# A one-core transformer kernel: opening, loads, seams, query rotation, and mask and scores ahead of the turning

## The chip, the cores and the metric

The kernel runs on one core of one Trainium2 chip. The metric is the device time of one execution in microseconds; lower is better. Engines are TensorE (PE; its weight loads are shown as PEld), VectorE (DVE), ScalarE (ACT), GpSimd (POOL) and SyncE (SP). They run at once, each in the order of its own program, and wait for one another by semaphores.

## The reference

The input is one sequence of 512 tokens with 1024 features. The reference computes a chain of blocks, each with a residual: an HGRN mixer, a SwiGLU feed-forward, sparse attention (NSA) on shared keys and values, a second SwiGLU, and then a second stage with differential attention, a squared-ReLU feed-forward, a state-space layer (S5) and another feed-forward. The first layers are modulated: the condition c goes through silu and a matrix into gains and shifts.

```python
def modulate(x, gain, shift, scale):
    return rms_norm(x, gain) * (1 + scale[:, None, :]) + shift[:, None, :]
# NSA: q, keys and values by head; rope on q and on two of three key sets
s_c = einsum('bqhgd,bchd->bhgqc', qp, kc) * scale      # against compressed blocks
s_s = einsum('bqhgd,bqhkd->bhgqk', qr, ks_g) * scale   # against selected blocks
s_w = einsum('bqhgd,bkhd->bhgqk', qr, kw) * scale      # against a window
o = g[:, :, 0] * o_c + g[:, :, 1] * o_s + g[:, :, 2] * o_w
```

Compressed keys and values come from a two-layer MLP over blocks of 32 tokens (cmp_w1, cmp_w2). With 512 tokens all eight selectable blocks are selected and the window covers the sequence, so both are causal attentions.

## The kernel before

Activations lie transposed: 8 tiles of 128 features by 512 tokens. Every large product is computed as three products of rounded parts: weights are split into whi (ScalarE, a rounding copy, L388) and wlo (VectorE, the rest, L392), activations into hh and hl. Weights come in blocks of 1 MB on SP's queue, two buffers deep. A *segment* is one matrix (h_q, h_f, h_v, h_g, h_out, ffn0_in0, ...); its blocks are processed in turn, and each engine has a body per block. PSUM banks 0 to 3 serve two blocks alternately. Between two segments whose results are taken by different engines, `boundary` on TensorE waits until every result of the segment before has been taken: ahead of the first block (L2665) where the new segment reads the same activations, behind it (L2677) where it waits for new ones.

The modulation columns of later layers are computed alongside: for each block ScalarE issues a load into `ada_ring` (L489), VectorE adds eight slices weighted by silu(c) (`ada_sums`, L509 and L513), and TensorE sums over partitions (`ada_products`, L473). In a segment's last block `ada_sums` goes before the eviction, and `ada_products` before the sums of squares.

*Opening.* Modulation columns of the first norm: 8 slices of ada_w (SP's queue). VectorE accumulates 12 of 16 columns (L527, L530), TensorE computes 4 by 128x1 products (L547) and closes the 12 by 12 products with ones (L559). x comes last on ScalarE's queue (2 MB). TensorE turns it (L2632); ScalarE squares (L2185) and copies (L2186) each turned tile; TensorE sums squares with a matrix of ones (L538). The gain, the norm's factor and the shift give hh and hl.

*NSA projections.* Segments n_kvc (2 blocks), n_ks, n_vs, n_kw, n_vw (1 each), n_q (4). Before n_kvc ScalarE issues `nsa_loads` (L655 to L667): rope tables, masks, gate weights, both cmp_w1 (2 MB each) and cmp_w2. Hooks `n_hook_pe`, `n_hook_act`, `n_hook_dve` run after block nb (n_kvc 0 and 1, n_ks 2, n_vs 3, n_kw 4, n_vw 5, n_q 6 to 9). POOL swaps half heads by small DMAs for the rotation.

*Query rotation.* Queries are eight tiles, in four pairs. `query_pieces(b)` are five VectorE steps on 1024 columns (L754, L757, L761, L766, L769): times sine, times cosine, add, times the norm's factor, and the same factor on the unrotated query. Pairs 0, 1, 2 run in the hooks 7, 8, 9, and the five pieces of pair 3 in attention steps 4 to 8. The factor of all lies in `xn`.

*Attention.* 68 steps: per key head one compressed step and two query pairs x four token tiles (t = 3 to 0) x two branches, with (t+1) x 128 keys. Step w consists of mask (L869) and scores (L887; L881 for compressed) on TensorE, a maximum on VectorE (L1113), exp on ScalarE (L1007), weighting on VectorE (L1100), turning on TensorE (L899), a copy on ScalarE (L995, L991), and products with values on TensorE (L919). They are pipelined: in iteration w TensorE does turn(w-3), mask(w), scores(w), values(w-4). Scores alternate between two bank pairs, so mask(w) waits for exp(w-2); the turned tiles have one bank pair, so turn(w) waits for copy(w-1). ScalarE does copy(w-3), then exp(w); VectorE maximum(w), then weighting(w-1).

## Time and profile before

| | |
|---|---|
| median of 3 runs | 2970.71 us (2970.0 to 2975.85) |
| the profiled execution's own time | 2976.58 us |
| its span, first to last instruction | 2974.8 us |
| PE busy (share of the span) | 2788.4 us (94%) |
| DVE busy | 1643.8 us (55%) |
| ACT busy | 1059.9 us (36%) |
| POOL busy | 100.4 us (3%) |
| chain that ended last | PE 62%, issue 23%, DVE 9%, DMA 3%, ACT 2% |
| mean granted TensorE clock | 0.971 |

All views are of the one profiled execution, and times inside are counted from its first instruction. Matmul busy times overlap a little, since they are pipelined: "busy" for TensorE is an upper figure. A row of the timeline ends, where the engine stood idle before it, with the idle time and what ended it. "L899" is line 899 of the kernel; tiles that were carved out of one tensor have its name (nsa_area, s_area, h_area).

### The profile page before, as it was taken

How to read it: one execution, taken by the hardware profiler on the slowest of the kernel's cores; microseconds unless marked ns; L12 is line 12 of the kernel's file. 1: busy time of each engine (PE TensorE's matmuls, PEld its weight loads, DVE VectorE, ACT ScalarE, POOL GpSimd, SP SyncE). 2: the span in 40 equal slices, each digit the busy share in tenths (PEclk: the TensorE clock that was granted, in tenths of full speed). 3: DMA queues.
4: the chain of work that ended last, by engine and by line, in shares of the span. 5: the costliest groups of instructions: out<-in, count | busy, mean ns of one | idle time of the engine just before them, and what ended most of it. 6: DMA issues, size and time to landing. Idle time of an engine off the chain costs nothing.

```text
span 2974.8 us, 38309 instructions
## 1 busy us (share of the span) xinstructions
PE 2788.4 (94%) x14746; PEld 2238.9 (75%) x14746; DVE 1643.8 (55%) x2350; ACT 1059.9 (36%) x1559; POOL 100.4 (3%) x135
## 2 busy tenths in 40 slices
PE   5999999999979899999999998899999968999999
PEld 4898778888668556788887775788887757778787
DVE  4566566766436776533334557477777394353342
ACT  3312233222323565332233448332341524342231
POOL 2004000000011000000000100000000000000000
PEclk9999999999989999999999999999999988999999
DMA  5640346565363100333333420144444661323232
GB/s 209 199 148 1 105 136 198 149 197 157 105 182 107 43 1 15 97 88 96 94 87 110 126 79 1 57 101 134 141 143 150 231 108 64 92 85 99 85 99 71
DMA packets 402088, 326.36 MB, mean 110 GB/s; under 512 B 14920, under 2 KB 387360, under 8 KB 400928
## 3 DMA queue, kind: packets, MB, share of 16 engines
q1 hardware_dynamic: 319936, 232.80, 26.7%
q10 hardware_dynamic: 77376, 80.07, 8.4%
q0 software_dynamic: 4640, 11.60, 1.5%
q8 instruction: 95, 1.56, 0.2%
q14 instruction: 41, 0.34, 0.0%
HBM read 293.05 MB, written 19.86 MB: 105 GB/s over the span
## 4 chain that ended last, share of the span: by engine, by line
PE 62%; issue 23%; DVE 9%; DMA 3%; ACT 2%; POOL 1%; ACTq 1%; DVEq 0%; POOLq 0%
PE ps L451 44%; PE ps L429 3%; PE ps L445 2%; PE ps L433 1%; DVE ada_acc L1781 1%; DMA ada_ring<-in_ada_w 1%; PE ps L899 1%; DVE ada_ring L513 1%; PE ps L919 1%; PE ps L1649 1%; PE ps L2648 1%; PE ps L887 1%; DVE h_area L1783 1%; DVE h_area L1785 1%; DMA xin<-in_x 1%
## 5 line engine op out<-in xcount | busy, mean ns | idle before, releaser
L451 PE MATMUL ps<-hh,whi 128*128 128x512 f32 x1744 | 693.5, 398 | 5.0 <-DVE xT L2484 1.6
L451 PE MATMUL ps<-hh,wlo 128*128 128x512 f32 x1744 | 681.7, 391 | 0.0
L451 PE MATMUL ps<-hl,whi 128*128 128x512 f32 x1744 | 681.1, 391 | 0.0
L392 DVE TENSOR_TENSOR wlo<-raw,whi 128x2048 fp32r<-128x2048 f32 x198 | 453.9, 2292 | 364.7 <-ACT whi L388 364.7
L388 ACT ACTIVATE whi<-raw 128x2048 fp32r<-128x2048 f32 x198 | 377.6, 1907 | 381.5 <-PE ps L451 250.9
L451 PEld LDWEIGHTS ps<-hh,whi 128*128 128x128 f32 x1744 | 329.1, 189 | 80.0 <-issue 11.9
L451 PEld LDWEIGHTS ps<-hl,whi 128*128 128x128 f32 x1744 | 329.2, 189 | 71.6 <-issue 4.5
L451 PEld LDWEIGHTS ps<-hh,wlo 128*128 128x128 f32 x1744 | 328.8, 189 | 69.7
L451 PE MATMUL ps<-hid_h,whi 128*128 128x512 f32 x756 | 306.7, 406 | 0.0
L451 PE MATMUL ps<-hid_l,whi 128*128 128x512 f32 x756 | 298.4, 395 | 0.0
L451 PE MATMUL ps<-hid_h,wlo 128*128 128x512 f32 x756 | 298.4, 395 | 0.0
L451 PEld LDWEIGHTS ps<-hid_h,whi 128*128 128x128 f32 x756 | 141.8, 188 | 37.8 <-issue 4.3
L451 PEld LDWEIGHTS ps<-hid_l,whi 128*128 128x128 f32 x756 | 141.8, 188 | 37.4 <-issue 4.3
L451 PEld LDWEIGHTS ps<-hid_h,wlo 128*128 128x128 f32 x756 | 141.7, 187 | 34.6
L513 DVE SCALAR_TENSOR_TENSOR ada_ring<-ada_ring,cact 128x256 f32<-128x256 f32 (+1 forms) x336 | 151.8, 452 | 12.1
L2227 ACT ACTIVATE sq<-xT 128x512 f32 (+1 forms) x56 | 35.4, 632 | 292.8 <-DVE xT L2484 139.4
L2482 DVE TENSOR_TENSOR xT<-xT,ps 128x512 f32 (+1 forms) x40 | 27.4, 687 | 163.1 <-PE ps L451 142.6
L2290 ACT ACTIVATE hid_h<-hid_f 128x512 f32 (+1 forms) x44 | 27.8, 633 | 246.9 <-DVE hid_f L2530 246.9
L2368 ACT ACTIVATE act_t<-ps 128x512 f32<-128x512 f32 x64 | 38.0, 598 | 198.4 <-PE ps L451 189.5
L429 PE MATMUL ps<-hh,whi 128*128 128x512 f32 x176 | 77.1, 438 | 32.6 <-ACT hh L2210 32.6
L2582 DVE TENSOR_TENSOR hid_f<-act_t 128x512 f32<-128x512 f32 x64 | 43.5, 688 | 102.8 <-ACT act_t L2368 102.4
L2530 DVE TENSOR_TENSOR hid_f<-act_t,ps 128x512 f32<-128x512 f32 x44 | 30.2, 686 | 126.6 <-PE ps L451 121.7
(413 smaller groups left out, 4076.0 us busy)
## 6 DMA issues: line engine op xcount, KB each, us to landing
raw<-in_ffn_w_in SPq DMA_DIRECT2D x44, 1024.0 KB, 6.0
ada_ring<-in_ada_w ACTq DMA_DIRECT2D x82, 512.0 KB, 4.4
raw<-in_ffn_w_up SPq DMA_DIRECT2D x32, 1024.0 KB, 5.3
raw<-in_ffn_w_down SPq DMA_DIRECT2D x32, 1024.0 KB, 5.6
raw<-in_ffn_w_out SPq DMA_DIRECT2D x32, 704.0 KB, 4.5
raw<-in_hgrn_w_in SPq DMA_DIRECT2D x16, 1024.0 KB, 5.6
raw<-in_attn_w_qkv SPq DMA_DIRECT2D x12, 1024.0 KB, 5.1
s_area<-cp_dram SPq DMA_DIRECT2D x6, 2048.0 KB, 9.0
```

The lines of the kernel that those rows point to most:

```text
L388: nc.scalar.activation(whi[:, par, :], raw[:, par, :], ACT.Copy).then_inc(w_hi, 1)
L392: nc.vector.tensor_tensor(wlo[:, par, :], raw[:, par, :], whi[:, par, :].bitcast(F32), ALU.subtract).then_inc(w_lo, 1)
L429: nc.tensor.matmul(ps[:, 2 * par + j, :], tile(w, kt, j), hi[:, kt, :], start=(kt == 0 and n == 0), stop=False)
L433: m = nc.tensor.matmul(ps[:, 2 * par + j, :], tile(wh, kt, j), lo[:, kt, :], start=False, stop=(kt == k - 1))
L445: m = nc.tensor.matmul(ps[:, bank, half * 256:half * 256 + 256], x[:, kt, t0:t0 + P], w[:, kt, :], start=(kt == 0 and n == 0), stop=(kt == ...
L451: m = nc.tensor.matmul(ps[:, bank, :], tile(w, kt, j), x[:, kt, :], start=(kt == 0 and n == 0), stop=(kt == k - 1 and n == 2))
L513: nc.vector.scalar_tensor_tensor(out=acc if last else w[:, 0, :], in0=w[:, kt, :], scalar=cact[:, kt:kt + 1], in1=w[:, 0, :], op0=ALU.mult ...
L887: m = nc.tensor.matmul(ps[:, S_BANK[w % 2] + i, 0:n], nqr[rows, p, t * P:(t + 1) * P], (k_sel, k_win)[br][rows, p // 2, 0:n], start=False, ...
L2227: nc.scalar.activation(sq[:, q:q + 1, :], xT[:, bass.ds(b * s.dve + j, 1), :], ACT.Square).then_inc(sq_rdy, 1)
L2368: nc.scalar.activation(act_t[:, j, :], ps[:, 2 * par + j, :], ACT.Relu).then_inc(ev_a, 1)
L2530: nc.vector.tensor_tensor(hid_f[:, par, :], act_t[:, par, :], ps[:, 2 * par + 1, :], ALU.mult).then_inc(ev_v, 1)
L2582: nc.vector.tensor_tensor(hid_f[:, j, :], act_t[:, j, :], act_t[:, j, :], ALU.mult).then_inc(hidf_rdy, 1)
```

## The change

1. *Opening.* x is loaded first, on SP's queue. TensorE turns x first, with the narrow products of slices 0 and 1 between. Squares are taken from the untransposed x by ScalarE, one row per token with a running sum (`accum_out`); VectorE spreads the four columns over a diagonal after its fourth slice, and TensorE sums with four 128x128 products. The closing products are split: 4 columns for the gain first, then 8 for the shift in another bank. VectorE computes the gain, two normalised tiles, then shift and the first wlo.
2. *Loads.* Both cmp_w1 and cmp_w2 leave `nsa_loads` and are issued after block 1 of n_kvc.
3. *Seams.* `boundary` is always put behind the first block of a segment; before it, only evictions up to the last block are awaited. In the last block of a segment with a norm behind it `ada_sums` goes behind the eviction, and `ada_products` behind the sums of squares.
4. *Query rotation.* Pair 1 runs in hook 9, pairs 2 and 3 in attention steps 1 to 10, and the factors lie in separate places.
5. *Attention.* In iteration w mask and scores go ahead of the turning.

```diff
@@ ada_first_dve, behind the slice kt
+                if kt == 3:
+                    first_square_spread(dve)
...
+        def first_square_spread(dve):
+            for t in range(TT):
+                dve.wait_ge(x_sq, t + 1)
+                nc.vector.tensor_scalar(rstd[:, t * P:(t + 1) * P], ident[:, :], x_ssq[:, t:t + 1], None, ALU.mult
+                                        ).then_inc(sq_rdy, 2)
+        def first_square_sums(pe):
+            for t in range(TT):
+                pe.wait_ge(sq_rdy, 2 * t + 2)
+                nc.tensor.matmul(ps[:, 7, t * P:(t + 1) * P], ones[:, :], rstd[:, t * P:(t + 1) * P], start=True, stop=True,
+                                 skip_group_check=True).then_inc(ssq_rdy, 2)
...
-            for j in range(NV):
-                m = nc.tensor.matmul(ps[:, 4, j:j + 1], ada_sum[:, j * P:j * P + P], ones[:, 0:1],
-                                     start=False, stop=True, skip_group_check=True)
-            m.then_inc(ada0_used, 1)
+            for bank, part in ((4, range(KT, NV)), (6, range(KT))):
+                for j in part:
+                    m = nc.tensor.matmul(ps[:, bank, j:j + 1], ada_sum[:, j * P:j * P + P], ones[:, 0:1],
+                                         start=(j == 0), stop=True, skip_group_check=True)
+                m.then_inc(ada0_used, 1)
@@ head_rstd
-            if n >= 6:
-                act.wait_ge(hn_rdy, n)
+            if n == 8:
+                act.wait_ge(hn_rdy, 6)
...
+        Q_RS = [xn[:, :, :], nqr[:, 4:6, :], xn[:, :, :], sq[:, :, :]]
@@ attention_pe
-                if w == 3:
-                    pe.wait_ge(ev_a, after(seg["n_q"])[1])
-                if 0 <= w - 3 < NS:
-                    turn(w - 3)
                 if w < NS:
...
                     scores(w)
                 if w == 1:
                     last_query_sums()
+                if w == 3:
+                    pe.wait_ge(ev_a, after(seg["n_q"])[1])
+                if 0 <= w - 3 < NS:
+                    turn(w - 3)
@@ n_hook_act
+            if nb == 1:
+                cmp_loads(act)
@@ nsa_act, before the copy of step 2
+                    if w == 5:
+                        act.wait_ge(hn_rot, 10)
@@ n_hook_dve
-            if nb >= 7:
-                for piece in query_pieces(dve, nb - 7):
+            if nb in (7, 9):
+                for piece in query_pieces(dve, (nb - 7) // 2):
                     piece()
@@ nsa_dve
-                if 4 <= w < 9:
-                    last_query[w - 4]()
+                if 1 <= w < 11:
+                    last_queries[w - 1]()
@@ ScalarE, opening
-                if kt >= 2:
-                    act.wait_ge(ssq_rdy, kt - 1)
-                nc.scalar.activation(sq[:, kt % 2, :], ps[:, kt % 4, :], ACT.Square).then_inc(sq_rdy, 1)
                 nc.scalar.activation(xT[:, kt, :], ps[:, kt % 4, :], ACT.Copy).then_inc(ev_v, 1)
+                if kt % 2:
+                    t = kt // 2
+                    if t >= 2:
+                        act.wait_ge(x_sq, t - 1)
+                    nc.scalar.activation((sq, xn)[t % 2][:, :, :].rearrange("p s n -> p (s n)"), xin[:, t, :], ACT.Square,
+                                         accum_out=x_ssq[:, t:t + 1]).then_inc(x_sq, 1)
@@ VectorE, linear
-                    ada_sums(dve, s, b, par)
+                    late = s.name in norm_after and isinstance(b, int) and b == s.n - 1
+                    if not late:
+                        ada_sums(dve, s, b, par)
                     evac(b, par)
+                    if late:
+                        ada_sums(dve, s, b, par)
@@ TensorE, linear
-                if change and need is None:
-                    boundary(pe, s)
-                elif change:
+                if change:
...
-                    if change and need is not None and isinstance(b, int) and b == 1:
+                    if change and isinstance(b, int) and b == 1:
                         boundary(pe, s)
```

On ScalarE, in the order of its program, this stands before n_kvc and in it before the change (L489 is the modulation load, L2249 the eviction, L388 the rounding of a weight block):

```order
L657 DMA nsa_area<-in_k_rope 128x1280
L658 DMA nsa_area<-in_k_nsa 128x772
L659 DMA nsa_area<-in_nsa_w_q 128x8x48
L661 DMA nsa_area<-in_cmp_w 128x16x256
L662 DMA nsa_area<-in_cmp_w 128x16x256
L664 DMA nsa_area<-in_cmp_w 128x2x64 x2
L666 DMA nsa_area<-in_cmp_w 128x2x64
L489 DMA ada_ring<-in_ada_w 128x8x128
L2249 ACTIVATE nsa_area<-ps 128x512 x2
L388 ACTIVATE whi<-raw 128x2048
```

And this after the change, down to the eviction of n_ks (L2344, L2345):

```order
L672 DMA nsa_area<-in_nsa_w_q 128x8x48
L489 DMA ada_ring<-in_ada_w 128x8x128
L2275 ACTIVATE nsa_area<-ps 128x512 x2
L388 ACTIVATE whi<-raw 128x2048
L489 DMA ada_ring<-in_ada_w 128x8x128
L2275 ACTIVATE nsa_area<-ps 128x512 x2
L388 ACTIVATE whi<-raw 128x2048
L677 DMA nsa_area<-in_cmp_w 128x16x256
L678 DMA nsa_area<-in_cmp_w 128x16x256
L680 DMA nsa_area<-in_cmp_w 128x2x64 x2
L682 DMA nsa_area<-in_cmp_w 128x2x64
L2344 ACTIVATE sq<-ps 128x512
```

Five issues have moved from ahead of the first modulation load to behind n_kvc's second conversion and ahead of n_ks's eviction.

On TensorE two iterations of the attention (t falls from 3 to 0; L899 turns, L869 is the mask, L887 scores, L919 values) read before:

```order
L899 MATMUL ps<-ident,nsa_area 128x128 x6
L869 MATMUL ps<-mask_r 128x128 x2
L887 MATMUL ps<-nsa_area 128x256 x2
L919 MATMUL ps<-nsa_area 64x128 x8
L899 MATMUL ps<-ident,nsa_area 128x128 x6
L869 MATMUL ps<-mask_r 128x128 x2
L887 MATMUL ps<-nsa_area 128x128 x2
L919 MATMUL ps<-nsa_area 64x128 x6
```

And after, with L887 the mask, L905 scores, L917 the turning and L937 values:

```order
L887 MATMUL ps<-mask_r 128x128 x2
L905 MATMUL ps<-nsa_area 128x128 x2
L917 MATMUL ps<-ident,nsa_area 128x128 x6
L937 MATMUL ps<-nsa_area 64x128 x6
L887 MATMUL ps<-mask_r 128x128 x2
L905 MATMUL ps<-nsa_area 128x128 x2
L917 MATMUL ps<-ident,nsa_area 128x128 x4
L937 MATMUL ps<-nsa_area 64x128 x6
```

The turning now stands between the scores of a younger step and the values of an older one.

On VectorE, from the attention's first maximum on (L1113; L1100 weights, L754 is a step of pair 3), before:

```order
L1113 TENSOR_REDUCE nsa_area<-ps 128x2
L1096 RECIPROCAL nsa_area<-nsa_area 128x2
L1097 TENSOR_TENSOR nsa_area<-nsa_area 128x2
L1100 TENSOR_SCALAR nsa_area<-nsa_area 128x384 x2
L754 TENSOR_TENSOR h_area<-h_area,nsa_area 128x1024
```

And after, one iteration of the second step of the attention (L1135 is the maximum, L1122 weights, L775 is a step of pair 2):

```order
L1135 TENSOR_REDUCE nsa_area<-ps 128x2
L1118 RECIPROCAL nsa_area<-nsa_area 128x2
L1119 TENSOR_TENSOR nsa_area<-nsa_area 128x2
L1122 TENSOR_SCALAR nsa_area<-nsa_area 128x512 x2
L775 TENSOR_TENSOR nsa_area<-nsa_area 128x1024
```

The rotation steps begin in iteration 1 instead of 4 and there are ten of them instead of five.

## Rows read from the trace of the kernel before

**Rows 1.** Timeline, opening: start, duration, engine, line, operation, operands, count, idle before, releaser

```profile
15.01 0.46 PE L2625 MATMUL ps<-ident,vec_a 120*128 120x120 f32 x1 [15.01 <-DMA ones<-in_k_ones]
...
29.99 1.82 DVE L530 SCALAR_TENSOR_TENSOR ada_sum<-ada_first,cact,ada_sum 128x1536 f32<-128x1536 f32 x1 [1.34 <-DMA ada_first<-in_ada_w]
...
31.00 0.59 ACT L2186 ACTIVATE xT<-ps 128x512 f32<-128x512 f32 x1
...
47.49 5.26 PE L559 MATMUL ps<-ones,ada_sum 128*128 128x1 f32 x24
...
53.13 2.28 DVE L392 TENSOR_TENSOR wlo<-raw,whi 128x2048 fp32r<-128x2048 f32 x1
...
57.04 0.77 PE L429 MATMUL ps<-hh,whi 128*128 128x512 f32 x1 [4.30 <-ACT hh L2210]
```

**Rows 2.** Stretches: length, busy PE PEld DVE ACT POOL, clock, DMA share, GB/s

```profile
16.00:29.00 13.00, 3.58 (x16) 3.49 (x16) 11.93 (x7) 1.31 (x2) 0.00 (x0) 1.00 1.01 414
```

**Rows 3.** Timeline of the key/value projections: DMA issues and waits behind them

```profile
828.27 7.89 ACTq L664 DMA_DIRECT2D nsa_area<-in_cmp_w  x2
...
836.87 1.17 ACTq L489 DMA_DIRECT2D ada_ring<-in_ada_w  x1
...
844.24 0.28 DVE L509 TENSOR_SCALAR ada_ring<-ada_ring,cact 128x128 f32<-128x128 f32 x1 [20.52 <-DMA ada_ring<-in_ada_w]
...
852.41 0.58 PE L473 MATMUL ps<-ones,ada_acc 128*128 128x1 f32 x2 [4.53 <-DVE ada_acc L513]
```

**Rows 4.** Stretch in TensorE's pause, columns as in rows 2

```profile
842.00:844.00 2.00, 0.00 (x0) 0.00 (x0) 0.00 (x0) 1.98 (x2) 0.00 (x0) 0.50 1.04 272
```

**Rows 5.** Stretches: first and second group of the sparse attention

```profile
992.00:1036.60 44.60, 39.28 (x314) 25.21 (x314) 34.93 (x87) 30.84 (x83) 0.00 (x0) 0.89 0.01 1
1036.60:1081.20 44.60, 40.95 (x380) 27.32 (x380) 31.79 (x88) 30.41 (x85) 0.00 (x0) 1.00 0.01 1
```

**Rows 6.** TensorE's waits in the second group: sum us, times, longest us

```profile
PE ps L899 <- ACT nsa_area L995: 1.8, 4, 0.7
PE ps L899 <- ACT nsa_area L991: 1.2, 1, 1.2
PE ps L899 <- DVE nsa_area L1087: 0.7, 1, 0.7
```

**Rows 7.** Timeline of ScalarE, a 1024-wide activation of the query norm

```profile
957.82 1.06 ACT L726 ACTIVATE xn<-xn 128x1024 f32<-128x1024 f32 x1
```

**Rows 8.** Chain of waits, n_ks and n_kw on TensorE: start, us, what

```profile
852.99 13.76 PE ps L451 x48
...
881.50 10.91 PE ps L451 x48
```

**Rows 9.** Chain of waits at a seam, from mlp0_out0 to mlp0_in1

```profile
2783.81 3.05 PE ps L451 x13
...
2788.13 1.90 PE ps L451 x7
```

**Rows 10.** Timeline of VectorE at the end of h_out

```profile
419.99 1.41 DVE L2445 SCALAR_TENSOR_TENSOR xn<-xT,gains_a,rstd 128x512 f32<-128x512 f32 x2
```

**Rows 11.** Timeline at the attention's start and in its first steps

```profile
990.96 0.68 DVE L1074 TENSOR_REDUCE nsa_area<-ps 128x16 f32<-128x512 f32 x1
...
1001.09 1.09 PE L899 MATMUL ps<-ident,nsa_area 128*128 128x128 f32 x8 [2.70 <-ACT nsa_area L991]
...
1004.02 0.96 DVE L1113 TENSOR_REDUCE nsa_area<-ps 128x2 f32<-128x768 f32 x1 [3.44 <-PE ps L887]
...
1005.95 1.22 DVE L754 TENSOR_TENSOR h_area<-h_area,nsa_area 128x1024 f32<-128x1024 f32 x1
```

**Rows 12.** Chain of waits: widest values, turn and scores at full clock

```profile
1094.33 1.07 PE ps L899 x8
...
1097.19 1.02 PE ps L919 x16
...
1105.56 1.06 PE ps L887 x4
```

More of the change, by code:

```diff
@@ L531, in ada_first_dve @@
                                                    op0=ALU.mult, op1=ALU.add).then_inc(ada0_sum_v, 1)
+                if kt == 3:
+                    first_square_spread(dve)
             dve.wait_ge(cols_ps, 2)
             link(nc.vector.tensor_copy(cols_b[:, 0:NROW_B], ps[:, 5, 0:NROW_B]))
-        def first_square_sum(pe, kt):
-            pe.wait_ge(sq_rdy, kt + 1)
-            nc.tensor.matmul(ps[:, 7, :], ones[:, :], sq[:, kt % 2, :], start=(kt == 0),
-                             stop=(kt == KT - 1)).then_inc(ssq_rdy, 1)
+        x_ssq = gains_a[:, 4, 0:TT]
+        def first_square_spread(dve):
[8 more added lines that the diff above has]
+                                 skip_group_check=True).then_inc(ssq_rdy, 2)
         def ada_first_pe(pe, k0, k1):
@@ L787, in n_hook_pe @@
                 pe.wait_ge(ada_rdy, seg["n_kvc"].ada_seg + 1)
-                pe.wait_ge(nsa_in, 64)
+                pe.wait_ge(nsa_in, 48)
                 head_square_sums(pe, 0, after(seg["n_ks"])[1])
@@ L966, in n_hook_act @@
                 nc.scalar.activation(gates.rearrange("p t n -> p (t n)"), ps[:, 7, 0:192], ACT.Copy).then_inc(gate_rdy, 1)
-                head_rstd(act, 6, xn[:, :, :])
+                head_rstd(act, 6, Q_RS[1])
             if nb == 9:
-                head_rstd(act, 8, xn[:, :, :])
+                head_rstd(act, 8, Q_RS[2])
         def nsa_act_seam(act, link):
@@ L1010, in nsa_act @@
                 if w == 2:
-                    head_rstd(act, 10, xn[:, :, :])
+                    head_rstd(act, 10, Q_RS[3])
         def nsa_dve_round(dve):
@@ L1032, in n_hook_dve @@
             if nb == 2:
-                dve.wait_ge(nsa_in, 64)
+                dve.wait_ge(nsa_in, 48)
                 link(nc.vector.tensor_reduce(small[:, 1:2], rotm, AX.X, ALU.add))
@@ L1101, in weighted @@
                 ins.then_inc(at_p, 1)
-            last_query = query_pieces(dve, 3)
+            last_queries = query_pieces(dve, 2) + query_pieces(dve, 3)
             for w in range(NS + 5):
@@ L1153, in d_hook_pe @@
             if db == 1:
-                pe.wait_ge(nsa_in, 96)
+                pe.wait_ge(nsa_in, 80)
             if 1 <= db <= 8:
@@ L1291, in diff_dve_start @@
             s = ROWS["attn_subln_2"]
-            dve.wait_ge(nsa_in, 96)
+            dve.wait_ge(nsa_in, 80)
             lv = lam_vec.rearrange("p (a b n) -> p a b n", a=2, b=2)
@@ L2086, in _ @@
         def _(sp):
+            sp.dma_start(xin[:, :, :], a["x"][0].rearrange("(t p) d -> p t d", p=P)).then_inc(x_in, 16)
             for kt in range(FIRST):
@@ L2423, in _, with first_shift @@
             dve.wait_ge(cols_rdy, 1)
-            link(nc.vector.tensor_tensor(mods[:, 0:16], ps[:, 4, 0:16], cols_a[:, 0:16], ALU.add))
-            modulated_gain(0, ROWS["norm_mix"], 8).then_inc(mods_rdy, 1)
-            if upto >= 2:
+            link(nc.vector.tensor_tensor(mods[:, 8:16], ps[:, 4, 8:16], cols_a[:, 8:16], ALU.add))
+            link(modulated_gain(0, ROWS["norm_mix"], 8))
+            def first_shift():
+                dve.wait_ge(ada0_used, FIRST + 2)
+                nc.vector.tensor_tensor(mods[:, 0:8], ps[:, 6, 0:8], cols_a[:, 0:8], ALU.add).then_inc(mods_rdy, 1)
                 convert_lo(dve, segs[0], 0, 0, 0)
@@ L2447, in apply @@
                                                    op0=ALU.mult, op1=ALU.mult).then_inc(xn_rdy, 1)
+                    if j == 0 and kt == 1:
+                        first_shift()
                     if kt:
@@ L2498, in _ @@
             if upto >= 2:
-                dve.wait_ge(mods_rdy, 1)
                 apply(0, 0, *mod_cols(0), FIRST_UNITS)
@@ L2631, in _ @@
                 for t in range(TT):
-                    m = nc.tensor.transpose(ps[:, kt % 4, t * P:(t + 1) * P], xin[:, t, kt * P:(kt + 1) * P],
-                                            ident[:, :])
+                    m = nc.tensor.transpose(ps[:, kt % 4, t * P:(t + 1) * P],
+                                            xin[:, t, kt * P:(kt + 1) * P], ident[:, :])
                 m.then_inc(mm, 1)
-                if kt:
-                    first_square_sum(pe, kt - 1)
-            first_square_sum(pe, KT - 1)
+                if kt % 4 == 3:
+                    ada_first_pe(pe, kt // 4, kt // 4 + 1)
+            ada_first_pe(pe, 2, 4)
+            first_square_sums(pe)
             def square_sums(s, m, b, par):
```

24 lines of the change are left out of this document (12 added, 12 removed).

## The prediction, made before the changed kernel was run

> **What bounds the kernel now.** I read the page's engine shares, then the chain of waits, then the stretches where TensorE stands still, and in those the timeline of all engines. TensorE is busy for nearly the whole span, so only time in which it waits, or runs at the lower clock, can be won. The change touches four such places.
>
> In the opening TensorE does not start the first weight block until 57.04 [rows 1]. Between 16 and 29 us the DMA engines move 414 GB/s [rows 2], so the stretch ends with a transfer: VectorE adds the last of eight slices of the first modulation weights at 29.99. All else follows serially: x is turned, squared and summed on TensorE, and only then come the 24 narrow products from 47.49 to 52.75, a full VectorE conversion (53.13 to 55.41), and the first products.
>
> In the key/value projections ScalarE stands at its own DMA issues, 7.89 us for one line. The modulation load behind them is issued at 836.87, VectorE waits 20.52 us for it, and TensorE resumes at 852.41 [rows 3], having fallen to half the clock while it stood (0.50, that is 1.2 GHz [rows 4]).
>
> Between segments with different evacuators TensorE waits for the last eviction. In the sparse attention it is busy 40.95 of 44.60 us in a steady group [rows 5], and its waits there stand before the turning [rows 6].
>
> **The opening.** x moves to the head of SP's queue, its turning goes before the weight products, squares are taken row by row on ScalarE, and only 4 of 12 late columns are wanted before the gain. The first 30 us still carry the same bytes: x (2.1 MB) and eight slices (8.4 MB), 10.5 MB, which at 414 GB/s is 25.4 us; with about 2 us until the first data and as much for landing the last slice is there at about 29.4. It was used at 29.99. So the last VectorE addition ends at about 31.4, or later if something else stops VectorE: the new spread of squares stands after its fourth slice. ScalarE needs for it eight copies at about 0.5 apart and four squares of 1024 columns with their sums, about 1.25 each by the 1.06 of a 1024-wide activation [rows 7], 9.0 us together, starting some 2.4 us after the constants land. If they land at 12 instead of 15, squares end at 23.4, the spread at 24.3, four additions of 1.82 later it is 31.7. If at 15, 34.7. I take 31.7, since x's small rows now precede the large ones. Then 8 of the 24 narrow products (5.26/24 = 0.22 each) make 1.8, the two VectorE steps 0.5: gain at 34.0. Two normalisations run while the other 16 products end at 37.0. The shift and the conversion (2.28) end at about 39.8, where 55.41 stood. The move of the conversion behind two normalisations costs nothing, since it waits for the shift anyway. The products, whose high parts are then there, and VectorE's first low part start at about 39.9, where TensorE started at 57.04 and the low part at 56.9: 17.0, of which I take **16.5 us**, as the constants may be a little later than 12. Bounds: 13 (constants at 15) and 19 (nothing but the last slice binds).
>
> **The loads.** The two large compression weights and three small ones leave ScalarE's queue ahead of n_kvc and are issued after its second block. Left ahead are three loads; the first modulation load is issued at 824 instead of 836.87 and lands behind 1.25 MB at about 831. Then 2.9 us of VectorE sums, 2.3 of conversion for n_ks, 2.9 of the second sums: 839.2, and the product. n_ks starts at 839.7 instead of 852.99: 13.3. It needs 11.0, about what n_kw takes at full clock (10.91), instead of 13.76 [rows 8], if TensorE stands only 2 us: 2.8. Two waits for ScalarE's evictions (n_vs, n_vw) go, 2.5 as two seams of 1.27 [rows 9]. Together **18.6 us**. The moved issues hold ScalarE for about 10 to 12 us from 843 on. Behind them stand n_ks's evictions and the conversion for n_kw. TensorE meanwhile runs n_ks to 850.7 and, as it no longer waits for those evictions, n_vs to 862.5 and its sums to 864.2. By my bookkeeping ScalarE is free at about 856, n_kw's low weights are there at 862.8: 1.4 us spare. If that cover is gone, each us late is a us lost; bounds 11 and 20. Compression's own weights are wanted by VectorE only at about 872.
>
> What speaks against it is contention: the rows show ScalarE held until 836.87 while 4.2 MB move [rows 3], and now POOL's 2 MB of copies and n_kw's 1 MB of weights start inside the same stretch.
> The Trainium skill (DMA: Bandwidth & Descriptors, "Issuing engines are not separate DMA queues") says that transfers of all issuing engines run on the same 16 DMA engines and interleave. By that rule the moved bytes delay n_kw's weights, and the term would be some 4 us smaller; without it 18.6 stands. The same rule leaves the last opening slice where it is. By that rule 414 GB/s is what all queues share; the trace agrees, with a DMA share of 1.01 in that stretch [rows 2].
>
> **Segment seams.** Outside the NSA part the wait for all evictions moves behind the first block for h_v, ffn0_in1, ffn1_in1, d_v and both second mlp inputs. A seam of this kind is 2786.86 to 2788.13, 1.27 us [rows 9]; I count 1.3, 0.7, 1.5, 1.0, 1.3, 1.3: **7.1 us**, bounds 4 and 8. In h_out the last eviction goes ahead of 4.1 us of modulation sums that now run beside the squares; but VectorE still has sums, conversion (2.29) and then the gain in a row from about 411.4: normalising at 418.2 instead of 419.99 [rows 10]: **1.8 us** (0 to 4). In n_out TensorE's last block binds: nothing.
>
> **Query rotation.** Of twenty full-width VectorE steps of 1.22, before the attention now stand those of query pair 1 where those of pair 2 stood, so it still starts at the same point relative to the projection (990.96 before [rows 11]). Pair 2's five steps, 6.1 us, join pair 3's in the first ten attention steps. The stretch that pair 1 leaves stays empty. In the attention's first group VectorE then has, per widest step, a maximum as wide as a rotation step (1.2), a weighting of about 1.3 and 1.2 of rotation, 3.7, against about 3.3 on TensorE (turn 1.07, mask 0.11, scores 1.06, values 1.02 [rows 12]; the mask is my estimate for two short ones).
>
> **Mask and scores ahead of the turning.** A turn waits until ScalarE has copied the turn before it; mask(w) waits only for exp(w-2), which ScalarE does earlier. So scores now fill those waits. In a steady group they sum to 1.8 + 1.2 + 0.7 = 3.7 us [rows 6]. Followed: at the group's head scores(3) fills the 0.7 wait, but scores(4) then waits 0.9 for exp(2); values(2) ends 1.5 us earlier. At the second head pair three smaller waits shrink by 1.1. So 2.6 per group, three groups: 7.8. In the first group the old order had a 2.70 wait at the turn and 3.44 on VectorE [rows 11]; the new one wins about 1 us by step 8, then VectorE with its ten rotations binds and gives back 2: I count +1.0. Sum: **6.8 us** gained; bounds: 14 (all waits of four groups gone, no loss) and a loss of 4 (VectorE binds all ten steps, nothing gained later).
>
> Sum: 16.5 + 18.6 + 7.1 + 1.8 + 6.8 = 50.8. The profiled execution took 2976.58 (span 2974.8, 1.8 around it); less 50.8 is 2925.8. Against the median 2970.71 of the runs, 5.87 below it, that is **2920**.
>
> **Rivals.** (1) The load stall moves instead of going: ScalarE, held behind the moved issues, evicts n_ks and converts for n_kw some 12 us late of TensorE. For: the 7.89 row [rows 3] and the copies in the same stretch. Against: TensorE has 22 us of work before it needs n_kw. Time 2920 + 12 = 2932. (2) The attention gains nothing: VectorE binds the first group by five more steps, and the waits reappear before the mask. For: 3.7 against 3.3. Against: 44.6 against 31.8 of VectorE in later groups [rows 5]. 6.8 + 4 less: 2931. (3) Slower than before: scores and turn become serial with ScalarE in every step. Turn(w-3) stands behind scores(w), copy behind the turn, exp(w) behind the copy, and the next mask behind that exp; with mask 0.11 and scores 0.74 on average (1.06 for the widest quarter, less in step for the others) 64 steps pay 0.85 each, 54 us: 2970.7 - 44.0 + 54 = 2981. It decides from the point at which such a round of two steps exceeds TensorE's work in two. Widest: 1.17 + 1.07 + 1.0 for the copy (1024 wide [rows 7]) + 1.5 for exp (estimate: two of 512, 0.59 each [rows 1], with their sums) = 4.7 against 6.5, so it should not. (4) More than forecast: every attention wait goes and the opening is bound by the last slice alone: 2920 - 9 = 2911.
>
> **How the numbers follow.** Forecast 0.67, (1) 0.12, (2) 0.10, (4) 0.08, (3) 0.03. The range 2907 to 2935 takes in (1), (2), (4) and the opening's bounds. A measurement of this kernel tells 0.2% (6 us) from no change; all cases but (3) are faster by more: faster 0.96, same 0.01, slower 0.03.
>
> **What would show it.** First weight product at 39 to 43; VectorE's last slice at about 32 and no wait for squares over 1 us. n_ks directly behind n_kvc within 3 us; full clock there; n_kw behind n_vs's sums. No eviction wait at seams. Groups of 42.0 us in the attention, the first 45.6. The forecast is wrong if the group stays at 44.6, if n_kw's conversion is late, or if the modulation load still lands after 836.

## The result, and the profile after

The changed kernel takes 2941.9 us (median of four runs, 2938.87 to 2944.53), the kernel before 2973.28 in its four (2970.0 to 2978.29): ratio 0.9893, interval 0.9874 to 0.9912. It is faster, by 31 us of medians and 35.6 us between the two profiled executions (span 2939.2 against 2974.8). The forecast was 2920, with 50.8 us gained, and its range ended at 2935. The direction was right; the gain between the profiles was forecast 15 us too large, and the time lies 7 us above the range.

The page of the changed kernel; TensorE was busy 94% of the span before:

```profile
span 2939.2 us, 38309 instructions
PE 2789.2 (95%) x14738; PEld 2235.6 (76%) x14738; DVE 1642.2 (56%) x2355; ACT 1056.4 (36%) x1559; POOL 101.0 (3%) x135
```

Since TensorE runs the same products in the same segments, the start of each segment's first product can be laid beside that of before. How much earlier it starts is the segment's shift, and the differences between such shifts are the terms of my sum. "Again" is the same kernel profiled once more.

| term, us gained | forecast | changed | changed again |
|---|---|---|---|
| opening | 16.5 | 16.4 | 16.3 |
| h_out | 1.8 | 1.8 | 1.8 |
| seams: h_v, ffn0_in1, ffn1_in1, d_v, mlp0_in1, mlp1_in1 | 7.1 | 0.6+0.85+1.7+0.1+0.2+1.45 = 4.9 | 5.0 |
| loads, n_kvc to n_vw | 18.6 | 12.3 | 13.6 |
| attention | 6.8 | 2.3 | 0.7 |
| all between these | 0 | -2.1 | -4.6 |
| sum | 50.8 | 35.6 | 32.8 |

The 0.2 at mlp0_in1 is read from the second profile (0.22); in the first the shift rises by 2.1 us a segment earlier and falls by 2.8 there, and hides it.

**Opening.** The chain of waits where TensorE starts (start, us, what), and then the timeline of TensorE and VectorE ahead of it:

```profile
38.24 0.17 DVE mods L2455
38.40 2.21 DVE wlo L392
...
40.66 2.08 PE ps L429 x4
```

```profile
13.33 0.46 PE L2659 MATMUL ps<-ident,vec_a 120*128 120x120 f32 x1 [13.33 <-DMA ones<-in_k_ones]
...
24.29 0.29 DVE L543 TENSOR_SCALAR rstd<-ident,gains_a 128x128 f32<-128x128 f32 x1 [1.72 <-ACT xn L2211]
...
31.05 1.82 DVE L530 SCALAR_TENSOR_TENSOR ada_sum<-ada_first,cact,ada_sum 128x1536 f32<-128x1536 f32 x1 [0.90 <-DMA ada_first<-in_ada_w]
```

These answer to [rows 1]. The constants land at 13.3 (I took 12), the spread ends at 24.6 (24.3), the addition of the last slice ends at 32.9 (31.7), the conversion ends at 40.6 (39.8), TensorE starts at 40.66.

**Loads.** ScalarE's timeline around its issues, which answers to [rows 3]:

```profile
803.39 0.59 ACTq L489 DMA_DIRECT2D ada_ring<-in_ada_w  x1
...
817.73 3.65 ACTq L678 DMA_DIRECT2D nsa_area<-in_cmp_w  x1
...
821.41 18.41 ACTq L680 DMA_DIRECT2D nsa_area<-in_cmp_w  x2
839.85 2.19 ACTq L682 DMA_DIRECT2D nsa_area<-in_cmp_w  x1
842.08 0.60 ACT L2344 ACTIVATE sq<-ps 128x512 f32<-128x512 f32 x1 [22.45 <-issue]
...
844.19 3.73 ACT L388 ACTIVATE whi<-raw 128x2048 fp32r<-128x2048 f32 x2
```

And the chain of the same stretch, which answers to [rows 8]:

```profile
819.69 11.03 PE ps L451 x48
830.72 11.52 PE ps L445 x96
...
844.32 1.81 ACT whi L388
846.15 2.30 DVE wlo L392
...
848.70 12.66 PE ps L451 x48
```

n_ks starts at 819.69 (852.99 before), n_vs directly behind it, and then TensorE stands from 842.24 to 848.70, but for four products (L733, sums of squares), which take 1.72 us there in the kernel before and in loads_on_sp. ScalarE's queue was held by the two small issues of L680 for 18.41 us, by all from 817.3 to 842.0; n_ks's eviction, whose products ended at 831, and the rounding for n_kw waited behind them. n_kw then took 12.66 us where it had taken 10.91: the granted clock had fallen while TensorE stood, and n_kw ran its first 3.2 us at half of it.

The hold in both kernels, from the first large issue to the end of the last small one (columns as in [rows 2]), before and then changed:

```profile
823.60:836.90 13.30, 13.30 (x61) 11.00 (x60) 0.12 (x1) 0.00 (x0) 0.00 (x0) 1.00 1.05 336
```

```profile
817.30:842.00 24.70, 22.71 (x147) 20.78 (x146) 4.14 (x8) 2.33 (x2) 8.30 (x16) 1.00 1.06 296
```

The DMA engines are full in both. Before, 4.5 MB move, all of ScalarE's queue; now 7.3 MB do, of which 2.1 are SP's and 1.7 POOL's.

**Attention.** A group is the 17 steps of one key head, counted from its first mask to that of the next (the last one to n_out's first product). Before, the four take 56.99, 44.62, 44.63 and 47.79 us; the second and third, which agree, are the steady ones. So the 44.60 that [rows 5] calls the first group is a stretch that starts 12.8 us into the first group of 56.99, and the forecast's 45.6 for the first group has no counterpart in this count. Stretches of the first and second group (length, busy PE, PEld, DVE, ACT, POOL, clock, DMA share, GB/s), which answer to [rows 5]:

```profile
960.00:1003.70 43.70, 38.03 (x310) 22.67 (x312) 39.45 (x91) 30.20 (x82) 0.00 (x0) 0.95 0.01 3
1003.70:1047.50 43.80, 42.27 (x380) 26.45 (x380) 31.49 (x88) 29.84 (x86) 0.00 (x0) 1.00 0.01 1
```

TensorE's waits in the second one (sum, times, longest), which answer to [rows 6]:

```profile
PE ps L887 <- ACT nsa_area L1029: 1.0, 2, 0.9
PE ps L917 <- ACT nsa_area L1017: 0.5, 1, 0.5
```

The waits fell from 3.7 to 1.5: 2.2 less, where 2.6 were forecast. Yet the group is 43.8, not 42.0: TensorE's busy time rose from 40.95 to 42.27 with the same 380 products. Where that sits is seen in three rows of each kernel. The changed one:

```profile
1021.18 0.88 PE L917 MATMUL ps<-ident,nsa_area 128*128 128x128 f32 x6
1021.98 1.09 PE L937 MATMUL ps<-nsa_area 128*64 128x128 f32 x16
1023.01 0.29 PE L887 MATMUL ps<-mask_r 128*128 128x128 bf16 x2
```

and the kernel before, where the mask follows the turning:

```profile
1053.52 0.87 PE L899 MATMUL ps<-ident,nsa_area 128*128 128x128 f32 x6
1054.23 0.28 PE L869 MATMUL ps<-mask_r 128*128 128x128 bf16 x2
1054.44 0.70 PE L887 MATMUL ps<-nsa_area 64*128 64x256 f32 x4
```

From the first of six turns it is 0.80 until values (128*64) starts, 0.71 until a mask (128*128) does. Over two groups the last turn's start lies 0.202 ahead of values and 0.109 ahead of a mask, within 0.001. Values to turning was 0.204, values to mask is 0.205: nothing comes back. Sixteen such steps in a group cost 16 x 0.093 = 1.5, and 1.3 is what TensorE's busy time rose by. The mask is bf16 and values are not, but the type is not the reason: in the changed kernel a turn also stands 0.109 ahead of a float32 product of shape 128*128 (L924, in all four places of the two groups).

**Seams.** The chain in the last mlp. The seam of [rows 9] is mlp1_out0 to mlp1_in1 in this mlp, and not mlp0_out0 to mlp0_in1 as its heading says; where it had a stop of 1.27, the second row is now one unbroken piece:

```profile
2587.01 76.16 PE ps L451 x336
2674.36 165.46 PE ps L451 x720
```

In h_out normalising starts at 400.31 instead of 419.99 [rows 10], 17.8 of it brought along, 1.8 won there.

### The profile page after: what moved, and what is told of

The parts are those of the page before. It is cut to its first block, busy times and chain, and to the rows that moved or that the text cites. A ratio compares the mean times of both kernels' runs of the same rounds, so it can differ in the third digit from the quotient of the medians.

```text
span 2939.2 us, 38309 instructions
## 1 busy us (share of the span) xinstructions
PE 2789.2 (95%) x14738; PEld 2235.6 (76%) x14738; DVE 1642.2 (56%) x2355; ACT 1056.4 (36%) x1559; POOL 101.0 (3%) x135
## 4 chain that ended last, share of the span: by engine, by line
PE 66%; issue 22%; DVE 7%; ACT 2%; DMA 1%; POOL 1%; ACTq 0%; DVEq 0%; POOLq 0%; SPq 0%
PE ps L451 47%; PE ps L429 4%; PE ps L445 2%; PE ps L433 2%; DVE ada_acc L1803 1%; PE ps L2682 1%; PE ps L917 1%; PE ps L937 1%; PE ps L1671 1%; DVE h_area L1807 1%; DVE h_area L1805 1%; PE ps L1712 1%; DVE nsa_area L1135 1%; PE ps L905 1%; POOL kT L1883 1%
## 5 line engine op out<-in xcount | busy, mean ns | idle before, releaser
L388 ACT ACTIVATE whi<-raw 128x2048 fp32r<-128x2048 f32 x198 | 377.4, 1906 | 374.9 <-PE ps L451 257.5
```

What stands on the lines that cost most here:

```text
L388: nc.scalar.activation(whi[:, par, :], raw[:, par, :], ACT.Copy).then_inc(w_hi, 1)
```

## The experiments

Twelve kernels ran, the two reprofiled ones among them. They were measured in three sets, each beside the kernel before, whose median was 2973.5, 2975.9 and 2977.0 us in them. The ratio is to that kernel, and across sets the ratios are to be compared, not the medians. The interval of rep, 0.9872 to 0.9907, overlaps those of loads_on_sp, turn_first, rotation_back, mask_turn_scores, turn_last and sp_rot_turn_first, and touches that of x_behind; for these the reading rests on the stretch of the trace that the edit touches, and the total only agrees with it.

**rep**: the changed kernel, unaltered.

> The changed kernel once more, unaltered. Its purpose is a second profile: which of the milestones repeat. Theory: the stall of 6.5 us before n_kw's products (842.2 to 848.7), the steady attention groups of 43.8 us and the seams are fixed parts of the program and repeat within 0.3 us; the 2 to 3 us lost in the differential attention (13.7 us at half the clock where the kernel before showed 3.4) come from where the clock's windows fall and may move. Rival: the stall before n_kw is chance of the transfers and varies by several us. Time 2942 +- 2.

2942.34 us, 0.9889 (0.9872 to 0.9907). The gap ahead of n_kw is there again, at 5.0 us instead of 6.5 (n_ks took 12.7 us instead of 11.0, 3.4 us of it at half the clock, so TensorE came to it later; this is not within the 0.3 expected), steady groups 43.84 and seams are the same. The losses between the terms moved: the differential attention lost 2.8 us in the first profile and 0.7 here, the stage ahead of s_glu won 2.4 there and lost 3.5 here.

**before_again**: the kernel before, unaltered.

> The kernel before, unaltered, for a second profile. Theory: the parts that differ by 2 to 4 us from profile to profile (differential attention, the scans ahead of s_glu) are stretches of half clock that fall differently, and no loss by the change: in this profile they differ from the first one by as much, while the waits of the NSA loads and the attention groups repeat within 0.3 us. Rival: this profile agrees with the first everywhere, and then the 2 us missing in the second half belong to the change. Time 2973 +- 3.

2973.86 us, ratio 1.0 (0.9989 to 1.0012). The second profile ends 3.2 us earlier than the first. It is 2.9 us faster in the stage of the scans ahead of s_glu and 1.2 in n_ks, 1.4 us slower in the attention's first group (58.39 against 56.99), and its steady groups take 44.62 and 44.61 as in the first. So 2 to 4 us between two profiles of one kernel are scatter, and lie where TensorE stands often and the granted clock falls: the stage ahead of s_glu had 57.5 us at half the clock in the first profile and 48.2 in the second, and the whole span 174 and 171, against 166 and 179 for the changed kernel. The theory held for the steady groups, not for the loads to 0.3, and not for the differential attention, which agreed to 0.1 us.

That stage can be followed through all fourteen profiles. From d_v to d_out it shows 6.8, 10.2 or 17.1 us at half the clock, and against the first profile it loses at most 0.1 us with 6.8 (five profiles, both of before among them), 0.7 to 0.8 with 10.2 (six, rep among them) and 2.8 to 2.9 with 17.1 (three, the changed kernel's first among them). So the loss there goes with the clock; nine of the twelve profiles of changed kernels have it and neither of before, so a part of it may be the change's own. What makes the clock fall there was not found.

**loads_on_sp**: the five compression loads issued by SP behind its last key/value block.

```diff
-            if nb == 1:
-                cmp_loads(act)
@@ SP, after the segment's loads
+                if s.name == "n_vw":
+                    sp.wait_ge(ev_a, after(seg["n_kvc"])[1])
+                    cmp_loads(sp)
```

> The two large compression weights and the three small ones leave ScalarE's queue altogether; SP issues them after the last key/value weight block, behind the same point (both n_kvc blocks evicted). Theory: in the changed kernel ScalarE's queue stood 24.3 us at those issues (817.7 to 842.0), so n_ks was evicted and n_kw's weights converted too late; with ScalarE free n_kw's low weights are ready before n_vs ends and TensorE goes on at 842.3: 6 us less, and no half clock there (another 1.5): 2935. Rival: the 16 DMA engines are the limit (share 1.05 there), n_kw's raw weights or the copies of the window land just as late, or compression waits: gain under 2 us, 2940 to 2942.

2940.16 us, 0.9884 (0.9866 to 0.9901): faster than rep by 2 us in the median, by 3.9 in the span (2938.1 against 2942.0), and n_q starts 4.1 us earlier; the 6 to 7.5 expected did not come. SP's timeline and then TensorE's chain:

```profile
822.45 10.58 SPq L678 DMA_DIRECT2D nsa_area<-in_cmp_w  x1
833.07 11.20 SPq L680 DMA_DIRECT2D nsa_area<-in_cmp_w  x2
```

```profile
819.29 12.66 PE ps L451 x48
831.95 11.51 PE ps L445 x96
843.47 1.72 PE ps L733 x4
845.18 10.90 PE ps L451 x48
```

TensorE now runs through all four segments. The issues hold a queue as long as before (24.4 us, from 821.7 to 846.1, now SP's), in the same stretch, and TensorE waits for nothing there: SP issues its next weight block at 846.47, and ScalarE reads it at 857.18. So ScalarE's hold was the cause of the stall, and the shared transfers delayed nothing TensorE needs: VectorE waits 4.5 us for the compression weights, beside the products. The rival's mechanism falls, though the time of 2940 is the one it named.
The Trainium skill (DMA: Bandwidth & Descriptors, "Issuing engines are not separate DMA queues") says that all issuers share the DMA engines, and that spreading DMAs over issuers saves only the sequencer's time to start them, usually small relative to the DMA itself. The first half agrees: the DMA share is 1.06 in ScalarE's hold and 1.03 from 822 to 844 with the issues on SP. The second does not for this stretch: ScalarE's queue was held for 24.7 us, and the large loads took 24.6 from issue to landing.

**seams_back**: the wait for all evictions ahead of the first block again, where no normalisation precedes.

```diff
-                if change:
+                if change and need is None:
+                    boundary(pe, s)
+                elif change:
...
-                    if change and isinstance(b, int) and b == 1:
+                    if change and need is not None and isinstance(b, int) and b == 1:
```

> The changed kernel with the wait for all evictions back ahead of the first block wherever no normalisation stands between. Theory from the two traces: h_v gives back 1.3, ffn0_in1 0.8, ffn1_in1 1.8, mlp1_in1 1.5, and n_vs and n_vw 1.3 each where ScalarE is not late anyway; d_v and mlp0_in1 give nothing (other work of the step stood there). In all 5.4 to 8: 2948 to 2950. Rival: as I forecast blind, d_v 1.0 and mlp0_in1 1.3 too: 2950 to 2952; or the seams are given back at the next wait, under 3 us: 2944.

2956.5 us, 0.9928 (0.9914 to 0.9943): slower than rep by 12 us in the ratios and by 16.0 in the spans, both guesses short. TensorE's waits in the key/value projections, and the chain there:

```profile
PE ps L445 <- ACT nsa_area L2345: 12.1, 2, 10.9
```

```profile
826.13 16.70 ACTq L680
...
847.37 0.59 ACT nsa_area L2345
847.96 0.04 issue
848.00 13.60 PE ps L445 x96
```

By the shifts n_ks starts 4.7 us later than in rep and n_vs 15.7, so 11.0 are lost between them. From n_kvc to n_q this kernel wins 2.9 us where rep wins 13.7. ffn0_in1, ffn1_in1 and mlp1_in1 gain nothing any more. At h_v 2.2 us go, more than the seam's 0.6: 3.4 us of h_f run at half the clock here and none in rep. So the two edits hold each other up: without the moved seam, most of what the loads won is lost again to the held evictions. The gain at d_v falls from 0.11 to 0.00 and at mlp0_in1 from 0.22 to 0.05, so these two seams were worth 0.1 and 0.2; that products of the step's other work cover the evictions there is argued from the order of the program, not tested.

**turn_first**: the attention's order of before, the rotation as changed.

```diff
+                if 0 <= w - 3 < NS:
+                    turn(w - 3)
                 if w < NS:
...
                     mask(w)
                     scores(w)
...
-                if 0 <= w - 3 < NS:
-                    turn(w - 3)
```

> The changed kernel with the attention's order of before (turn, mask, scores, values); the query rotation stays moved. Theory: steady groups return from 43.83 to 44.6 us, the four together 2.3 to 3 us longer: 2944.5. Rival: the rotation, not the order, made the difference: groups stay at 43.8 and the time at 2942.

2947.37 us, 0.9907 (0.989 to 0.9923). Steady groups 44.61, as in before to 0.01. But the first group takes 60.89, where before took 56.99 and 58.39 with the same order: moving pair 2 into the attention costs 2.5 to 3.9 us in this pair of kernels. TensorE's waits in this first group:

```profile
PE ps L887 <- ACT nsa_area L1025: 5.8, 1, 5.8
PE ps L917 <- ACT nsa_area L1013: 3.9, 1, 3.9
PE ps L917 <- ACT nsa_area L1017: 3.4, 3, 1.3
```

**rotation_back**: pairs 0, 1 and 2 ahead of the attention again, the order as changed.

```diff
-            if nb in (7, 9):
-                for piece in query_pieces(dve, (nb - 7) // 2):
+            if nb >= 7:
+                for piece in query_pieces(dve, nb - 7):
...
-            last_queries = query_pieces(dve, 2) + query_pieces(dve, 3)
+            last_queries = query_pieces(dve, 3)
```

> The changed kernel with the query rotation where it stood before: pairs 0, 1 and 2 before the attention, pair 3 in its steps 4 to 8, one tile for the scale. The mask and scores stay ahead of the turning. Theory: moving pair 2 into the attention cost 3 to 4 us in its first group (turn_first: 60.9 against 57.0 of the kernel before, with the same order) and nothing is won before it; so the first group falls to 53 to 54.5, steady groups stay 43.83: 2938.5 to 2939.5. Rival: VectorE's five steps delay the attention's start by as much, as the forecast had it the other way round: start 3 to 4 us later, time 2942.

2937.66 us, 0.9866 (0.9846 to 0.9885). First group 53.79 against 56.6 and 58.2 in the changed kernel, steady groups 43.83; the attention begins at the same distance from n_q's first block (57.46 in both). Two stretches of one group's length together, of which the first starts 10.6 us after the first mask:

```profile
955.75:985.00 29.25, 24.03 (x177) 13.56 (x178) 26.52 (x59) 18.99 (x50) 0.00 (x0) 0.86 0.01 1
985.00:1009.50 24.50, 23.69 (x218) 14.88 (x218) 17.73 (x49) 15.74 (x46) 0.00 (x0) 1.00 0.00 1
```

and of rep, from 10.5 us after its first mask:

```profile
955.90:985.00 29.10, 23.02 (x154) 13.87 (x154) 27.05 (x53) 16.19 (x42) 1.45 (x4) 0.77 0.07 19
985.00:1014.10 29.10, 27.28 (x244) 16.45 (x240) 22.62 (x60) 18.32 (x52) 0.00 (x0) 1.00 0.01 1
```

VectorE is busy for 26.5 and 27.05 of the first 29 us, more than any other engine, and TensorE gets through 177 products there with pair 2 out of the way, 154 with it. TensorE stands more with it, and has 0.77 of the clock there against 0.86. The rival, a later start of the attention, falls.

**mask_turn_scores** and **turn_last**: two more orders. The first puts turn(w - 3) between mask(w) and scores(w); the second is

```diff
                     mask(w)
                     scores(w)
...
+                if w >= 5:
+                    values(w - 5)
...
                 if 0 <= w - 3 < NS:
                     turn(w - 3)
...
-                if w >= 4:
-                    values(w - 4)
```

> The changed kernel with a third order in each step: mask, turn, scores, values. Theory: each change between products of different tile shape (128*128, 64*128, 128*64) costs TensorE about 0.093 us (turn to values starts 0.202 apart, turn to mask 0.109); the order of before has three such changes in a step, the new one four, this one three. TensorE's busy time in a steady group falls from 42.27 by 16 x 0.093 = 1.5 back to 40.8; the waits rise a little, from 1.5 to 2.2, since the turn has only the mask ahead of it: group 43.0, 2 to 3 us less in all, 2939.5. Rival: the longer busy time has to do with something else, waits return as in the order of before (3.7): group 44.3 or more, 2943.5.

> The changed kernel with the order mask, scores, values (of one step earlier in number, w-5), turn. Theory (a change of tile shape costs TensorE 0.093 us): the turn again stands next to a mask (0.109) and not next to values (0.202), so three changes in a step, TensorE busy 40.9 in a steady group, and the waits stay as in the changed kernel at about 1.6, since the turn has as much ahead of it and values waits for a copy long done: group 42.4, four groups 5 to 6 us less, 2937. Rival: the later turn holds up VectorE and ScalarE (three slots of p) and waits grow by as much as is saved: group 43.8 or more, 2942 or more.

2944.38 us, 0.9898 (0.9881 to 0.9916), and 2939.69 us, 0.987 (0.9851 to 0.989). Steady groups 43.97 and 43.70. Both miss 43.0 and 42.4, and both show why in part. A stretch of one steady group's length in each, in this order:

```profile
1017.30:1061.20 43.90, 41.42 (x378) 26.11 (x378) 31.63 (x89) 30.36 (x85) 0.00 (x0) 1.00 0.01 1
```

```profile
1013.10:1056.80 43.70, 41.73 (x380) 26.98 (x379) 31.86 (x89) 29.83 (x85) 0.00 (x0) 1.00 0.01 1
```

TensorE's busy time falls from 42.27 to 41.42 and 41.73, and in turn_last the turn stands 0.109 ahead of the mask again: the cost of the change of tile shape is real. The fall is 0.85 and 0.54, though, where one change less in each of 16 steps should save 1.5; the rest is not explained. And idle rises from 1.5 to 2.5 and 2.0: most of what the order saves in busy time is waited for.

**sp_and_rotation**, **sp_rot_turn_last**, **sp_rot_turn_first**: the edits of loads_on_sp and rotation_back together, with the order as changed, that of turn_last, and that of before.

> Loads on SP and the rotation back where it was, together, the attention's order as changed. Theory: two separate places, so they add: 2940.2 less 3 to 3.5: 2937. Rival: the first attention group waits for what ends last in the projections anyway, the gains overlap: 2939 to 2940.

> Loads on SP, rotation back where it was, and the order mask, scores, values, turn. turn_last took 43.70 us in a steady group against 43.83 and 0.8 us more in the last: theory, the saved changes of tile shape are eaten by waits at the mask and the turn, so nothing is gained over sp_and_rotation: 2932 to 2933. Rival: in the first group, where VectorE no longer stands in the way, the saving comes through: 2930.

> As sp_and_rotation, but with the attention's order of before (turn, mask, scores, values): the order alone. Theory: steady groups 44.6, first group 57.0, last 47.8, as in the kernel before, 4 us over sp_and_rotation's 190.0 us of attention: 2936.7. Rival: the order wins only against the moved rotation; with the rotation back the first group is the same in both orders, and only 0.8 a steady group and 0.3 in the last remain: 2934.5.

2932.7 us, 0.9851 (0.9831 to 0.987); 2930.86 us, 0.9847 (0.9831 to 0.9863); 2938.56 us, 0.9872 (0.9855 to 0.9889). The two gains add: by the spans 3.9 and 6.6 us for each edit alone, 11.1 for both (2930.9 against rep's 2942.0), and by the ratios about 1.5, 7 and 11. Both of the first two beat the changed kernel, and are the best of all. The third isolates the order: first group 57.24 against 54.85 with the order as changed, steady groups 44.62 against 43.83, last stretch 47.79 against 47.51, together 4.3 us. One first group differs by up to 1.6 us between two profiles of a kernel, so the rival (first group alike) is to be judged by all of them: with the rotation back, the order as changed takes 53.79 and 54.85, that of before 56.99, 58.39 and 57.24. They do not overlap, and the rival falls. The same count bears on pair 2: with it in the attention, five profiles of the order as changed have 56.6 to 58.4, and the two without it 53.8 and 54.9. Between the first two kernels of this paragraph the intervals overlap; the profile has 53.43 + 2 x 43.71 + 48.29 = 189.1 for turn_last's order and 190.0 for the other.

**x_behind**: x from ScalarE's queue, behind the constants, as before.

```diff
@@ SP, at its head
-            sp.dma_start(xin[:, :, :], a["x"][0].rearrange("(t p) d -> p t d", p=P)).then_inc(x_in, 16)
@@ ScalarE, behind the load of ones
+            act.dma_start(xin[:, :, :], a["x"][0].rearrange("(t p) d -> p t d", p=P)).then_inc(x_in, 16)
```

> The changed kernel with x loaded from ScalarE's queue again, behind the constants, not from the head of SP's. Theory as in the blind forecast: squares and spread are set by x and the constants, the last slice by all 10.5 MB; x then comes later and the slices earlier. If x lands 3 us later, the spread of squares holds VectorE by about as much (it waited 1.7 us already), first products 2 to 3 us later: 2944.5. Rival: the last slice lands earlier by what x took ahead of it and makes it up: 2942.

2952.7 us, 0.9922 (0.9905 to 0.994): 10 us slower, both expectations wrong by a factor of three. Its timeline:

```profile
24.71 3.68 PE L2665 MATMUL ps<-ident,xin 128*128 128x128 f32 x16 [9.36 <-DMA xin<-in_x]
...
34.49 0.28 DVE L543 TENSOR_SCALAR rstd<-ident,gains_a 128x128 f32<-128x128 f32 x1 [1.72 <-ACT xn L2211]
34.70 7.58 DVE L530 SCALAR_TENSOR_TENSOR ada_sum<-ada_first,cact,ada_sum 128x1536 f32<-128x1536 f32 x4
```

x shares the DMA engines with slices already on the way and lands 21.1 us after its issue, not 8.7. VectorE's four spread steps wait for the squares of x and end at 34.8, where they ended at 24.6; it adds four slices only then, without waiting for any of them. The DMA engines also fall idle from 24 to 29 us. SP refills a slice's place when VectorE and TensorE have both used it; TensorE's narrow products stand behind the turning of x in its program, so SP issues the seventh slice at 29.38 instead of 18.79:

```profile
20.00:24.00 4.00, 0.00 (x0) 0.00 (x0) 2.65 (x2) 0.00 (x0) 0.00 (x0) 1.00 0.94 381
24.00:29.00 5.00, 4.29 (x23) 4.29 (x23) 0.28 (x1) 2.88 (x6) 0.00 (x0) 1.00 0.00 0
```

So more than half of the opening's 16.4 us (9.4 by the shift of h_q) hangs on x being first, as the spread stands in the middle of VectorE's slices.

## Why the forecast was right in direction and wrong in size

- **Opening, h_out: right**, to 0.2 us and 0.1 us, with every milestone within 1.3 us. My bound of 13 covered late constants and not a late x, and x late costs 9.4.
- **Loads: most of the term was right, one step failed.** n_ks starts 13.1 us earlier against n_kvc, where 13.3 was forecast. The step that failed is "The moved issues hold ScalarE for about 10 to 12 us from 843 on" and with it "ScalarE is free at about 856". Less the 20.2 us won by then, that is 823 to 836. They held it from 817.3 to 842.0: twice as long, and free 6.2 us later. The gap of 6.5 at n_kw holds 1.72 us of sums that the forecast had counted; beside loads_on_sp, which has no such hold, TensorE is 5.3 us later at n_kw and 6.5 at n_q, the rest by the lower clock (3.8 and 3.5 in rep). I had taken the length from 7.89 us [rows 3], part of a hold of 13.3 us in which 4.5 MB moved and none of it for another queue; here POOL's copies and two weight blocks shared the stretch, 7.3 MB in all. My rival 1 named this place at 12 us; it came at half its price or less. That ScalarE's hold was the cause, and not late transfers, loads_on_sp shows. It is also what the forecast had named as a sign of being wrong: n_kw's conversion came late.
- **Attention: two steps failed.** "So 2.6 per group": 2.2 of wait went in a steady one, but the new neighbourhood of turning and values costs 1.3 to 1.5, so 0.8 was left. I had treated an order as free for the engine that executes it. And "gives back 2": pair 2 in the first group costs 2.5 to 4.4, for nothing, since the attention starts no earlier without its five steps ahead of it (57.46 us after n_q's first product in all fourteen profiles). Rival 2 was right about VectorE in the first group and wrong about its price: it put the attention at 4 us lost, and it gained 2.3 and 0.7.
- **Seams: mis-sized.** I scaled the seams from the 1.27 of [rows 9], 0.7 to 1.5 each. Four measured 0.6, 0.85, 1.7 and 1.45; d_v and mlp0_in1, put at 1.0 and 1.3, measured 0.1 and 0.2. What the edit did between n_ks and n_vs I counted at 1.3, and without it 11.0 us are lost there, since ScalarE is held.
- **The rest**: I put it at nothing, and 2.1 and 4.6 us went between the terms. Two profiles of one kernel differ by 2.5 us there and by 2.9 in the stage ahead of s_glu; a single profile can't place a term of this size, and I had summed against one. The 0.7 and 2.8 us of it in the differential attention go with time at half the clock; the cause of that stays open.
- **The time.** The median is 21.9 us above 2920. Against its own profile the forecast was 2925.8, and the profiled execution took 2941.2: 15.4 of the 21.9. The terms give 15.2 of it: loads 6.3, attention 4.5, seams 2.2, the rest 2.1, opening 0.1. The other 6.5 come from the last step, which took the profiled execution to lie 5.87 above the median, from three runs; that of the changed kernel lies 0.7 below. The range's 15 us above the forecast held rival 1 or rival 2 alone, not halves of both and the seams at once: the misses all had one sign, since each term was taken with its cover intact.

## What to carry to other kernels

In this kernel a large DMA issue held the issuing engine for as long as the transfers around it took; put it on the queue whose next instruction is wanted last, and judge the hold by all bytes moving in that stretch, not by the same line elsewhere. When instructions are reordered to fill waits, list the pairs of neighbours before and after on the executing engine and look up each pair's distance in the timeline, as well as the waits. Work hidden under a long stretch of another engine costs nothing there; five short steps moved into a stretch where their own engine binds cost 2.5 to 4.4 us.

## What the runs showed of the chip that I had not expected

- Two neighbouring TensorE products of different tile shape start further apart: turn (128*128) to values (128*64) 0.202 us, turn to mask (128*128) 0.109, with the same turns; turn to scores (64*128) is 0.202 too, in mask_turn_scores. One such change more in each of 16 short steps was 3% of a group.
- Two issues of small loads (L680, 64 KB each) held a queue for 18.41 us, behind two of 2 MB just issued; on SP 11.20, with 10.58 on the second large one. In all, 24.7 us with 7.3 MB moving, 24.4 with 6.6 MB, and 13.3 with 4.5 MB before: in these three the hold goes with the bytes moving, not with the size of the instruction that stands.
- A 2 MB load issued 2.8 us later, from another queue, took 21.1 us to land instead of 8.7, with six slices of 1 MB issued ahead of it.
